# Compression in a hybrid attention and mixture-of-experts layer: first loads inside the projection, raw tiles by two queues, even tokens copied to a contiguous tile

## The reference, cut to what matters

```
xn = rms_norm(h, norm1_g)                      # 2048 tokens x 1024
proj = xn @ w_in                               # q, kc_r, vc_r, ks, vs, kw, vw, gates, ...

def compress_tokens(kv, pe, w1, b1, w2, b2):   # kv: 2048 tokens, G = 2 groups, HD = 64
    nc = (T - 32) // 16 + 1                    # 127 blocks of 32 tokens, one every 16
    idx = np.arange(nc)[:, None] * 16 + np.arange(32)[None, :]
    blk = kv[:, idx] + pe[:, None, :]
    blk = swapaxes(blk, 2, 3).reshape(B, nc, G, 32 * HD)
    h = gelu(blk @ w1 + b1)                    # 128 hidden
    return h @ w2 + b2

kc, vc = compress_tokens(kc_r, ...), compress_tokens(vc_r, ...)
y = nsa_attention(q, kc, vc, ks, vs, kw, vw, gates, slopes)
```

## Time and profile before

| | us |
|---|---|
| median of 3 runs | 3141.05 |
| lowest, highest | 3138.71, 3141.44 |
| profiled execution | 3138.34 |
| its span | 3136.5 |
| TensorE, VectorE, ScalarE, GpSimd busy | 2814.2, 1676.2, 1094.9, 1039.0 |

### The profile page before, as it was taken

One profiled execution on the slowest core, in us unless ns is written; L12 is line 12 of the kernel. 1 busy time (PEld: TensorE's weight loads), 2 busy tenths in 40 slices (PEclk: granted clock), 3 DMA queues, 4 the chain that ended last, 5 costly groups with the idle time before them and its releaser, 6 DMA issues. The chain is left out here.

```text
span 3136.5 us, 41105 instructions
## 1 busy us (share of the span) xinstructions
PE 2814.2 (90%) x14110; PEld 1925.3 (61%) x14111; DVE 1676.2 (53%) x3380; ACT 1094.9 (35%) x2270; POOL 1039.0 (33%) x996
## 2 busy tenths in 40 slices
PE   8989999999977699999989999999899999579980
PEld 5658888888865365665645556666444455456760
DVE  6655555655536666666666668788222222422227
ACT  0012222222215355555555456666211122123322
POOL 1267666866623402012131211100212333011116
PEclk9999999999987699999999989999899999789995
DMA  3332324322245101101010021100764243365848
GB/s 130 129 128 102 107 92 150 128 101 104 79 128 225 42 4 60 36 26 52 30 73 23 26 76 41 41 1 1 309 200 116 93 158 121 139 228 208 339 167 317
DMA packets 150215, 355.30 MB, mean 113 GB/s; under 512 B 13840, under 2 KB 61584, under 8 KB 143632
## 3 DMA queue, kind: packets, MB, share of 16 engines
q1 hardware_dynamic: 130016, 280.04, 25.8%
q0 software_dynamic: 13824, 50.34, 4.7%
q10 hardware_dynamic: 6192, 22.55, 1.8%
HBM read 230.52 MB, written 122.36 MB: 113 GB/s over the span
## 5 line engine op out<-in xcount | busy, mean ns | idle before, releaser
L546 ACT ACTIVATE p_kept<-p_a 128x256 f32<-128x256 f32 x336 | 128.6, 383 | 486.0 <-PE p_a L492 461.6
L1510 DVE CUSTOM_DVE_ANT_0 b_prob_s<-b_pq,b_sel 128x640 f32<-128x640 f32 (+5 forms) x192 | 168.7, 911 | 130.9 <-PE b_pq L1402 124.2
L1438 PE MATMUL b_po<-b_probT,vsw 128*64 128x256 f32 (+1 forms) x1824 | 232.4, 373 | 0.0
L1363 POOL TENSOR_TENSOR b_rate<-gates,b_total 128x256 f32<-128x256 f32 x64 | 37.9, 612 | 581.6 <-DVE b_total L1524 581.6
L1805 DVE CUSTOM_DVE_ANT_0 d_prob<-d_pq,d_bias 128x1024 f32<-128x1024 f32 (+6 forms) x192 | 168.0, 910 | 69.5 <-PE d_pq L1697 67.5
L1462 ACT ACTIVATE b_prob_s<-b_prob_s,b_neg 128x1152 f32<-128x1152 f32 (+15 forms) x128 | 152.7, 1194 | 128.5 <-DVE b_neg L1518 128.3
L1402 PE MATMUL b_pq<-ks,b_q 64*128 64x512 f32 (+3 forms) x688 | 166.6, 548 | 18.2 <-PEq L60 9.3
L1533 DVE COPY b_probT<-b_pt 128x512 f32<-128x512 f32 (+1 forms) x253 | 152.5, 629 | 47.5 <-PE b_pt L1425 47.3
L1697 PE MATMUL d_pq<-d_keys,d_q 64*128 64x512 f32 (+3 forms) x576 | 166.6, 563 | 4.6 <-DVE d_seg_max L1805 3.6
L1425 PE MATMUL b_pt<-ident,b_prob_s 128*128 128x128 f32 x1088 | 158.0, 282 | 7.5 <-DVE b_probT L1533 7.1
L1438 PEld LDWEIGHTS b_po<-b_probT,vsw 128*64 128x64 f32 x1824 | 107.6, 136 | 92.9 <-issue 55.3
(11 more groups left out here) (372 smaller groups left out, 6085.1 us busy)
## 6 DMA issues: line engine op xcount, KB each, us to landing
projT<-p_result SPq DMA_DIRECT2D x64, 512.0 KB, 2.8
y<-e_y ACTq DMA_DIRECT2D x43, 512.0 KB, 4.2
p_w<-in_wt SPq DMA_DIRECT2D x16, 1024.0 KB, 6.4
p_w_more<-in_wt SPq DMA_DIRECT2D x16, 1024.0 KB, 6.1
gates_T<-projT SPq DMA_DIRECT2D x64, 256.0 KB, 4.2
wgu<-in_w_gu SPq DMA_DIRECT2D x4, 4096.0 KB, 14.9
y<-b_q POOLq DMA_DIRECT2D x20, 512.0 KB, 21.6
p_xin<-in_x SPq DMA_DIRECT2D x16, 512.0 KB, 4.0
```

What stands on the lines that cost most here:

```text
L1438: mm = nc.tensor.matmul(po[u % 2][g * HD:(g + 1) * HD, o:o + w], s.vsw[:, kb, v0 + g * HD:v0 + (g + 1) * HD], probT[:, f % 4, g * w:(g + 1 ...
L1510: nc.vector.tensor_tensor_reduce(out=to, in0=pq[g][:, 0:nb * P], in1=away, scale=slopes[PAIRS * g + i], scalar=-3e38, op0=ALU.add, op1=ALU ...
```

## The change

The edits, each with its place:

- `t_projection`: at the start of unit 15, after the store of unit 14's last block, SP issues four loads of compression (`load_first`): the position terms, w1[0], and both halves of raw[0][0]. It first waits for products 3 and 4 of unit 14, and for the stores of T_KC and T_VC. raw[0][0] and w1[0] lie in the memory of `w`.
- The wait for all stores moves from the end of the projection's SP list to the end of SP's list in `compress`. `result` and `w` are kept until then.
- `compress`: SP issues the rows 0 to 63 of the other three raw tiles, ScalarE the rows 64 to 127, at the head of its list. There is no wait between the batches. The small constants now stand behind all raw tiles in SP's queue.
- ScalarE copies the even columns of each raw tile to `even[v][g]`, 128 x 8 x 128, one column offset after the other; the matmuls read 127 neighbouring elements of it.
- The sigmoid of the gates moves to the head of ScalarE's list in compressed attention, and VectorE's first gate waits for it.
- Tiles for raw, even and spread are laid over memory of later stages; the lists of semaphores that are cleared change with the edits (36 to 39 after the projection, 37 to 43 after attention).

```diff
+def load_raw(eng, d, to, v, g, shifted):
+    rows, at = slice(g * HD, (g + 1) * HD), slice(shifted * HD, (shifted + 1) * HD)
+    return eng.dma_start(to[at, 0:T - 1], d["qkT"][T_KC + v][rows, shifted:T - 1 + shifted])
...
@@ t_projection
+        sem = ctx.enter_context(phase_semaphores(nc, [*w_in, *spilled]))
+        result, stored = s.result, s.stored
...
+            def load_first():
+                sp.wait_ge(made[2], 7 * (ROUNDS - 1))
+                sp.wait_ge(made[3], 7 * (ROUNDS - 1))
+                for u in (1, UNITS + 1):
+                    for cols in range(2):
+                        slot, use = final_block(u, 0, cols)
+                        sp.wait_ge(stored[slot], 16 * (use + 1))
+                sp.dma_start(s.pe[:], d["cmp_pe"]).then_inc(s.pe_in, 16)
+                sp.dma_start(s.w1_first, d["cmp_w1"][0]).then_inc(s.w1_first_in, 16)
+                for shifted in range(2):
+                    load_raw(sp, d, s.raw_first, 0, 0, shifted).then_inc(s.raw_first_in, 16)
...
                     store(u - 1, 1, 0)
+                    if u == ROUNDS - 1:
+                        load_first()
...
-            for slot in range(NC):
-                sp.wait_ge(stored[slot], 16 * len([n for n in range(4 * ROUNDS) if n % NC == slot]))
@@ compress
+        later = s.b_sel[:].rearrange("p j g c -> p (j g c)")
+        raw = [[s.raw_first, later[:, 0:T]], [later[:, T:2 * T], later[:, 2 * T:3 * T]]]
+        w1 = [s.w1_first, ctx.enter_context(nc.sbuf_tensor("c_w11", [P, NJ, CMP_HIDDEN], fp32))[:]]
...
-            for v in range(2):
-                if v == 1:
-                    sp.wait_ge(raw_in[0][1], 32)
-                sp.dma_start(w1[v][:], d["cmp_w1"][v]).then_inc(w1_in[v], 16)
-                for g in range(GROUPS):
-                    rows = slice(g * HD, (g + 1) * HD)
-                    sp.dma_start(raw[v][g][0:HD, :], d["qkT"][T_KC + v][rows, :]).then_inc(raw_in[v][g], 16)
-                    sp.dma_start(raw[v][g][HD:P, 0:T - 1], d["qkT"][T_KC + v][rows, 1:T]).then_inc(raw_in[v][g], 16)
...
+            load_raw(sp, d, raw[0][1], 0, 1, 0).then_inc(raw_in[0][1], 16)
+            sp.dma_start(w1[1], d["cmp_w1"][1]).then_inc(w1_in[1], 16)
+            for g in range(GROUPS):
+                load_raw(sp, d, raw[1][g], 1, g, 0).then_inc(raw_in[1][g], 16)
...
+            for slot in range(NC):
+                sp.wait_ge(s.stored[slot], 16 * len([n for n in range(4 * 2 * UNITS) if n % NC == slot]))
...
-                pe.wait_ge(raw_in[v][g], 32)
+                pe.wait_ge(even_ready, 2 * v + g + 1)
                 for j in range(NJ):
-                    mm = nc.tensor.matmul(ph[2 * v + g][:, 0:NCMP], w1[v][:, j, :], raw[v][g][:, 2 * j:2 * j + span:CMP_STRIDE],
+                    b = j // (NJ // 2)
+                    mm = nc.tensor.matmul(ph[2 * v + g][:, 0:NCMP], w1[v][:, j, :], even[v][g][:, j % (NJ // 2), b:b + NCMP],
                                           start=(j == 0), stop=(j == NJ - 1))
...
         @block.scalar
+            for v, g in ((0, 1), (1, 0), (1, 1)):
+                load_raw(nc.scalar, d, raw[v][g], v, g, 1).then_inc(raw_in[v][g], 16)
+            for v in range(2):
+                for g in range(GROUPS):
+                    act.wait_ge(raw_in[v][g], 32)
+                    nc.scalar.activation(even[v][g], raw[v][g].rearrange("p (b r) -> p r b", r=CMP_STRIDE)[:, 0:CMP_STRIDE:2, :],
+                                         ACT.Copy).then_inc(even_ready, 1)
...
-            act.wait_ge(vsw_in, 16)
-            nc.scalar.activation(s.gates[:], s.vsw[:, :, V_GATE:V_DIFF], ACT.Sigmoid)
@@ compressed_attention
+            act.wait_ge(s.vsw_in, 16)
+            nc.scalar.activation(s.gates[:], s.vsw[:, :, V_GATE:V_DIFF], ACT.Sigmoid).then_inc(gates_ready, 1)
             exponentials(0)
...
+                if n == 0:
+                    dve.wait_ge(gates_ready, 1)
                 link(nc.vector.tensor_tensor(weight, rate, by, ALU.mult))
@@ program
+            w = kept_on.enter_context(nc.sbuf_tensor("p_w", [P, 2, 2, DT, P], fp32, side="right"))
...
                         compress(nc, d, s, sem)
+                        kept_on.close()
                         compressed_attention(nc, d, s, sem)
```

More of the change, by code:

```diff
@@ L41, in phase_semaphores @@
 @contextmanager
-def phase_semaphores(nc):
-    taken = []
+def phase_semaphores(nc, adopted=()):
+    taken = list(adopted)
     def named(name):
@@ L334, in t_projection @@
         outer = [sb(f"outer{k}", [P, 2, HK, P]) for k in range(3)]
-        result = [sb(f"result{k}", [P, 2, 512]) for k in range(NC)]
+        result, stored = s.result, s.stored
         kept = [[sb(f"kept{b}{k}", [P, QT]) for k in range(3)] for b in range(2)]
@@ L346, in t_projection @@
         x_in = [sem(f"p2_x_in{i}") for i in range(7)]
-        stored = [sem(f"p2_stored{k}") for k in range(NC)]
         free = xnT[:, 0:HK, HT:T]
@@ L2827, in program @@
             sums = [sb(early, f"token_sums{k}", [P, DT // 2, T // 2]) for k in range(4)]
-            w = sb(early, "p_w", [P, 2, 2, DT, P])
+            w = kept_on.enter_context(nc.sbuf_tensor("p_w", [P, 2, 2, DT, P], fp32, side="right"))
+            s.pe = kept_on.enter_context(nc.sbuf_tensor("c_pe", [P, 2, CMP_BLOCK // 2], fp32, side="right"))
+            spare = w[:].rearrange("p a b k c -> p (a b k c)")
+            s.raw_first, s.w1_first = spare[:, 0:T], spare[:, T:2 * T].rearrange("p (j h) -> p j h", h=CMP_HIDDEN)
+            s.raw_first_in, s.w1_first_in, s.pe_in = (nc.alloc_semaphore("c_" + n) for n in ("raw_first_in", "w1_first_in", "pe_in"))
+            s.stored = [nc.alloc_semaphore(f"p2_stored{k}") for k in range(6)]
             w_in = [nc.alloc_semaphore(f"p_w_in{b}") for b in range(2)]
@@ L2831, in program @@
             norm_and_v_projection(nc, d, s.ident, s.half, xnT, sums, w, w_in, spilled)
-            t_projection(nc, d, xnT, sums, w, w_in, spilled)
+            s.result = [kept_on.enter_context(nc.sbuf_tensor(f"p2_result{k}", [P, 2, 512], fp32, side="right")) for k in range(6)]
+            t_projection(nc, d, s, xnT, sums, w, w_in, spilled)
         s.logits = sb(ctx, "logits", [P, NT, NG + NG * NE])
```

43 lines of the change are left out of this document (21 added, 22 removed).

## The result

The changed kernel takes 3125.76 us (median of 5 runs, 3119.43 to 3127.18) against 3141.05 us (median of 5, 3138.71 to 3142.84): a ratio of 0.9946, interval 0.9931 to 0.996, so 12.6 to 21.7 us less. The forecast was 3129.5 with a range from 3124 to 3135.5: right in its direction and inside its range, with a gain of 15.3 us between the medians where the sum had 10.4.

A forecast was written before the change was run, and what follows sets the result against it. A stream of DMA transfers was taken to bound the hand-over from projection to compression and attention. 8.5 + 2.14 - 0.27 = 10.4 us off 3138.34 and 3141.05 gave 3127.9 and 3130.7, named 3129.5; range 3124 to 3135.5.

The forecast's parts named there:

- overlapping halves: Rival for compression's raw tiles: two queues write different halves at once, 2.5 us more gain, 12.9 us, 3127; chance 0.33.
- The bound: From the projection's end into compressed attention, a stream of DMA transfers sets the time, through `kw` and the `y` stall.
- The stores' wait: At the projection's end SP loses its 2.28 us wait; longer clears cost 0.14, so compression's first issue comes at 907.70.
- First loads for nothing: Four DMAs, 2.1 MB, issued in the projection's unit 15 into an empty queue, landing by 875, costed at nothing.
- What the stream loses: Compression's loads: w1[0] 2.6 us, raw[0][0] 4.7 us and the pause between batches 1.2 us, together 8.5 us.
- Two queues: Raw tile halves issued by SP and ScalarE in compression: gain 0 to 2.5 us, taken as 0.
- Contiguous even tokens: Compression: copies cost 1.02 us each, up to 2; 32 matmuls go from 7.0 to 6.8 or 3.4 us.
- Compute stays hidden, narrowly: Compress block's end: the compute chain ends at 30.1 to 34.7 us after first issue, SP's `kw` at 34.5.
- The sigmoid: Gates' sigmoid moved behind attention's barrier, 3.1 us with table loads, fits before the first exponential: cost 0 to 0.2 us.
- The clears: Semaphore clears at 0.045 us each: +0.14 us after the projection (36 to 39), +0.27 us after attention (37 to 43).
- The rival in which the shift isn't handed on: Clock changes in attention or sparse attention, or compute becoming the bound, absorb the gain: 3135 to 3141; chance 0.09.
- The two lower rivals: Early loads' waits come late in unit 15, 3137, chance 0.04; two queues hinder each other, 3150 at 90 GB/s, chance 0.04.

The follow-up runs named there:

- late_first: The changed kernel with its four early loads moved from the projection's last unit back to the head of SP's list in compression; 3134.96 us, ratio 0.9978.
- spread_loads: The changed kernel with late-needed loads moved to attention's head (cmp_dist, q chunks 2 and 3) or behind the stores of y (ks, kw, sparse attention's); 3117.56 us, ratio 0.9919.
- stores_wait: The changed kernel with SP waiting for all stores at the projection's end again; 3124.44 us, ratio 0.9951.
- no_pause: The kernel before, with only SP's wait for raw[0][1] ahead of the second batch of loads removed; 3138.09 us, ratio 0.9986.
- one_queue: The changed kernel with both halves of every raw tile issued by SP and none by ScalarE; 3128.12 us, ratio 0.9955.
- best: spread_loads with ScalarE issuing raw[0][0] and raw[0][1]'s upper half, SP the rest, raw[1][0] then small constants ahead of raw[1][1]; 3109.86 us, ratio 0.9905.
- strided: The changed kernel without ScalarE's four copies, the matmuls reading every 16th element of the raw tiles; 3129.98 us, ratio 0.9962.
- pad_one: The changed kernel with one redundant 0.5 MB half-tile load on SP's queue in the projection's last unit; 3131.73 us, one execution.

## Why the prediction was right, point by point

The stream and the stores' wait ahead of it, which make up the sum, were read rightly: 10.5 us measured to `y3`. That the median falls into the range owes something to luck. 15.3 us of gain lie outside the 8.5 to 11.5 to which the prediction gave 0.50, and 3125.76 is nearer to the 3127 that it wrote for overlapping halves, which did not happen; the range reached that far down for this rival only.

**The bound.** Right. The stretch was a stream of transfers, and its two ends (`kw` and the stall at `y`) set the time: late_first moves TensorE by 15 us and the end by 6 to 7, and spread_loads, which takes the loads away from both ends, gains 9 us more.

**The stores' wait.** Forecast 2.28 - 0.14, first issue at 907.70. Measured 3.55 us instead of 5.86 after the fold, so 2.3 us. In stores_wait it comes back with 2.1 to 3.0 us. Right.

**First loads for nothing.** Right within what can be told: they went at 864.68, as the queue and the engines were empty. The last fold ended between 903.45 and 905.89 in all traces, on average at 905.1 in the nine with early loads and at 904.7 in the five without, so that a cost of some tenths of a microsecond is not excluded.

**What the stream loses.** 8.5 us, of it 7.3 for the loads and 1.2 for the pause. Measured 8.3 us between first issue and attention (43.3 against 35.0, means of two); singly 6.2 to 7.0 (late_first) and 1.5 to 1.7 (no_pause). Right, each within 1.1 us.

**Two queues.** I took 0 in a range of 0 to 2.5 us and gave their overlap 0.33. The overlap did not happen: 240 instead of 224 GB/s, 7%. The Trainium skill, SBUF — State Buffer, "Can I just issue two DMAs to hit both halves?", has 6% for two such DMAs at once, and by this trace that agrees. The 0.8 us of gain that I had estimated by it did not come. The step that failed is the price of `w1[1]`: the sum had 2.6 us for it, 400 GB/s as if it were alone, and the working of the overlap gave the 2.1 MB around it 6.9 us, 304 GB/s. Beside half tiles in the other queue it went at their rate, 214 to 251 GB/s, and so two queues cost 0.6 to 1.4 us here (one_queue): below the range of 0 to 2.5, on the side that the prediction named only as a rival.

**Contiguous even tokens.** The copy was mis-sized: 1.94 us, not 1.02, for 1024 elements read with a stride of 64 bytes; it was the upper end that I had named. The matmuls came out near what was worked: 32 take 6.54 us at 1.2 GHz (6.8 forecast) and 3.84 us at the full clock (3.4 forecast; one_queue, best), against 7.0 to 7.2 with strides. The forecast took its prices from weight loads, which at the full clock were shorter than the matmuls here. "Compute stays hidden, narrowly": the chain ended 32.10 us after the first issue in a range of 30.1 to 34.7, and SP's `kw` at 34.04, where I had 34.5. strided confirms that the copies are only cover: without them compute ends last (34.80 where I had 34.2) and the time to `y3` is the same.

**The sigmoid.** Forecast 0 to 0.2 us. The first exponential starts 3.16 us after the barrier, before 3.17. Right, nothing lost.

**The clears.** The list at the projection's end: SP's wait went from 2.5 to 2.7 us, forecast +0.14. Behind attention 0.45 us where I had 0.27. Two things were off. The list there has 44 semaphores after the change, not 43: the traces have 37 clears in before and 44 in after. And one clear follows the other every 0.065 us (37 from 1074.3 to 1076.7 in before, 44 from 1066.6 to 1069.4 in after), where I had 0.045 from two barriers' whole waits. 7 times 0.065 is 0.45.

**What the prediction did not have.** It listed stages after 1077 that take another time as a sign that it was wrong, and that is what happened: the turning stage is 4.3 us shorter. The step that failed is the first one: "Nothing outside that place is edited", from which followed that nothing outside it would take another time. The edit moved three loads out of SP's queue; that changed how long SP is held by three issues 1300 us later, and the sum had no term for it. Without this the sum would have come to 10.1 us with the measured clears, 0.3 less than forecast, and the median near 3131. The median came out 3.7 us below the forecast, about the size of this stage, though the intervals of the full times are too wide to put the difference down to it.

**The clock.** The rival in which the shift isn't handed on got 0.09. The 3 us by which attention moves occur in both kernels alike and don't belong to the change. The two lower rivals are out as well: the early loads went at 864.68, and the half tiles did not fall to the 102 GB/s that a slower kernel needed.

## What to carry to other kernels

In a hand-over between stages, ask which transfer the barrier and the first reused buffer wait for, and count everything queued ahead of it: bytes that the next stage needs late belong behind the first stores (here 9 us), and bytes that it needs first belong into the quiet end of the stage before (here 6 to 7 us). A shorter chain of compute behind a stream of loads is only cover: `vc` came 2.0 to 2.6 us earlier in one_queue and moved the barrier by 0.6 to 1.4, while the 3 us that best took off the chain moved it by 3, since there the stream no longer ended last. After moving loads between queues, compare the stages far behind as well, since a queue's history can change how long an issue holds its engine.

## What the runs showed of the hardware

- Three issues of 1 MB loads held SP for 4.1 to 5.3 or for 8.1 to 9.1 us at the same place, depending on how many loads its queue had been given some 1300 us earlier; one more load of 0.5 MB was enough (pad_one).
- Two queues that write the two halves of tiles at once moved 237 to 240 GB/s together, where one queue moved 224; and a load to 128 partitions, alone at 382 GB/s, went at 214 to 251 beside them.
- A ScalarE copy of 1024 elements read at a stride of 64 bytes took 1.94 us; contiguous 256 and 512 elements took 384 and 595 ns.
- Clears of semaphores on GpSimd follow each other every 0.065 us (44 from 1066.6 to 1069.4 in after).
- TensorE's time for 127 columns read at that stride is 0.22 us at both levels of the granted clock; contiguous, 0.20 us at 1.2 GHz and 0.12 at 2.4 GHz (6.54 and 3.84 us for 32).
